# Seven block products, column-major, for the second merge gate's projection

## The reference

```
h = rms_norm(x, norm_g)
... , g_a, g_b = split(h @ w_in)          # g_a and g_b: 1024 columns each
y_a = gelu(u) * mixed(layer_norm(gelu(v))) * silu(z_a)
y_b = sparse_attention(q, k, v, qi, ki, wi) * silu(z_b)   # top 128 keys per query
o_a = y_a @ w_oa ;  o_b = y_b @ w_ob
merged = sigmoid(g_a + b_a) * o_a + sigmoid(g_b + b_b) * o_b
x = x + merged @ w_out
```

## Time and profile before

| | us |
|---|---|
| median of 3 runs | 794.5 (794.45 to 795.74) |
| the profiled execution, its own time | 794.48 |
| its span | 792.7 |
| PE busy | 783.3 (99%) |
| DVE busy | 587.6 (74%) |
| ACT busy | 353.7 (45%) |

### The profile page before, as it was taken

One profiled execution on the slowest core, in us unless ns is written; L12 is line 12 of the kernel. 1 busy time (PEld: TensorE's weight loads), 2 busy tenths in 40 slices (PEclk: granted clock), 3 DMA queues, 4 the chain that ended last, 5 costly groups with the idle time before them and its releaser, 6 DMA issues.

```text
span 792.7 us, 10745 instructions
## 1 busy us (share of the span) xinstructions
PE 783.3 (99%) x3836; PEld 659.2 (83%) x3836; DVE 587.6 (74%) x1026; ACT 353.7 (45%) x658; POOL 110.9 (14%) x101
## 2 busy tenths in 40 slices
PE   7999999999999999999999999999999999999998
PEld 6988888888888888888899888888888888888886
DVE  5779999978766763359986799999786658423895
ACT  6566644341444324434664765433324342335242
POOL 1257510000000000012211674000000000000130
PEclk9999999999999999999999999999999999999999
DMA  9634233223233122275873532323323222224574
GB/s 329 221 114 126 80 107 92 79 70 105 81 106 103 36 81 100 71 226 117 190 236 107 162 86 73 106 81 107 96 67 105 80 80 80 73 88 163 129 144 122
DMA packets 41572, 91.53 MB, mean 115 GB/s; under 512 B 2864, under 2 KB 3056, under 8 KB 41520
## 3 DMA queue, kind: packets, MB, share of 16 engines
q1 hardware_dynamic: 33408, 69.21, 27.8%
q0 software_dynamic: 7824, 21.06, 11.3%
q10 hardware_dynamic: 288, 0.59, 0.2%
HBM read 84.56 MB, written 6.29 MB: 115 GB/s over the span
## 4 chain that ended last, share of the span: by engine, by line
PE 91%; DVE 5%; DMA 2%; ACT 1%; issue 1%; ACTq 0%; DVEq 0%; SPq 0%
PE bank L700 22%; PE bank L702 22%; PE bank L701 22%; PE bank L784 4%; PE bank L736 3%; PE bank L735 3%; PE bank L734 3%; PE bank L674 2%; PE bank L692 2%; PE bank L630 1%; PE bank L683 1%; DMA x_sb<-in_x 1%; PE bank L645 1%; PE bank L644 1%; DVE w_lo L1149 1%; DMA norm_bc<-in_norm_g 1%
## 5 line engine op out<-in xcount | busy, mean ns | idle before, releaser
L1149 DVE TENSOR_TENSOR w_lo<-w_raw,w_hi 128x1024 fp32r<-128x1024 f32 x132 | 172.2, 1319 | 11.7 <-ACT w_hi L867 8.4
L700 PE MATMUL bank<-h_lo,w_hi 128*128 128x512 f32 x448 | 180.6, 403 | 0.0
L702 PE MATMUL bank<-h_hi,w_hi 128*128 128x512 f32 x448 | 174.7, 390 | 0.0
L701 PE MATMUL bank<-h_hi,w_lo 128*128 128x512 f32 x448 | 174.4, 389 | 0.0
L867 ACT ACTIVATE w_hi<-w_raw 128x1024 fp32r<-128x1024 f32 x132 | 135.6, 1056 | 22.3 <-DMA w_raw<-in_w_out 14.0
L700 PE MATMUL bank<-w_lo,h_hi 128*128 128x512 f32 x256 | 100.5, 393 | 0.0
L702 PE MATMUL bank<-w_hi,h_hi 128*128 128x512 f32 x256 | 99.9, 390 | 0.0
L701 PE MATMUL bank<-w_hi,h_lo 128*128 128x512 f32 x256 | 99.8, 390 | 0.0
L701 PEld LDWEIGHTS bank<-h_hi,w_lo 128*128 128x128 f32 x448 | 84.2, 188 | 18.5 <-issue 1.4
L700 PEld LDWEIGHTS bank<-h_lo,w_hi 128*128 128x128 f32 x448 | 84.2, 188 | 18.3 <-issue 1.4
L702 PEld LDWEIGHTS bank<-h_hi,w_hi 128*128 128x128 f32 x448 | 84.1, 188 | 18.1
(11 more groups left out here) (174 smaller groups left out, 1362.6 us busy)
## 6 DMA issues: line engine op xcount, KB each, us to landing
w_raw<-in_w_in SPq DMA_DIRECT2D x96, 512.0 KB, 3.7
w_raw<-in_w_out POOLq DMA_DIRECT2D x16, 512.0 KB, 6.1
w_raw<-in_w_out SPq DMA_DIRECT2D x12, 512.0 KB, 3.4
out<-x_sb POOLq DMA_DIRECT2D x4, 1024.0 KB, 6.4
w_raw<-in_w_oa SPq DMA_DIRECT2D x8, 512.0 KB, 3.4
w_raw<-in_w_ob SPq DMA_DIRECT2D x8, 512.0 KB, 3.3
x_sb<-out POOLq DMA_DIRECT2D x2, 2048.0 KB, 9.3
x_sb<-in_x SPq DMA_DIRECT2D x4, 512.0 KB, 9.1
```

The costliest lines, as they stand in the source:

```text
L700: nc.tensor.matmul(dst, s_h, m_l, start=(n == 0), stop=False)
L701: nc.tensor.matmul(dst, s_l, m_h, start=False, stop=False)
L702: last = nc.tensor.matmul(dst, s_h, m_h, start=False, stop=(n == len(pairs) - 1))
L1149: nc.vector.tensor_tensor(lo, w_raw[:, raw_slot(layer, u)], hi.bitcast(F32), ALU.subtract) \
```

## The change

The `gb` stage has 14 jobs instead of 8 (n = 48 to 61): seven products of blocks, each in two jobs p = 0, 1. h and the gate's weight are cut into 2x2 blocks (256 tokens or 512 channels a side). A job takes four blocks of 128 channels, two tiles of 128 gate columns and three passes: 24 matmuls with 256 moving columns, and fills one bank with two tiles of 256 tokens. The products are a11, a12, s5, s3, s6, s4, a22 in this order. The bank of a11 goes on to take s3, s4 and a22, the bank of a12 (its own after s5 opens it anew) takes s5 and s6. Between products ACT copies a bank to `g_b` (after a11, s5, s3), DVE adds a bank to `g_b` (after a12, s6, s4), and ACT makes the tanh in halves.

Four sums of blocks of h are made by DVE in ten steps (`h_sum_step`), one at the end of each `ga` job and of `oa` jobs 0 and 1. ACT rounds them in `oa` jobs 1, 3, 5, 7 and DVE makes their remainders in `oa` jobs 2, 4, 6 and `gb` job 0.

The stage takes 14 weight units instead of 8; eight of them are accumulated onto a slot by POOL. The roundings and remainders of the units, and those of the `ob` weights, stand in the jobs that `LATE_GATE_UNITS` and `OB_UNITS` list. Attention steps follow `gb` jobs 0, 2, 4, 6; y_b is split in `gb` jobs 8 to 10. Banks of `ob` and `out` are renumbered. The SBUF that software DMA uses for descriptors is cut to 4096 bytes a partition.

```diff
-    ("gb", "w_in", COL["gb"], 4), ("gb", "w_in", COL["gb"] + W512, 4),
+    ("gb", "w_in", COL["gb"], 14),
...
+SEVEN = 14
+UNIT_FIRST = np.cumsum([0] + [SEVEN if g[3] == SEVEN else NQ for g in GROUPS]).tolist()
+UNITS = UNIT_FIRST[-1]
...
+GATE_PRODUCTS = ["a11", "a12", "s5", "s3", "s6", "s4", "a22"]
+H_SUMS = ["s4", "s5", "s3", "s6"]
+H_ROUNDED = ["s5", "s4", "s3", "s6"]
+REGION = [0, 1, 0, 1, 0, 1, 0, 1, 0, 1, 0, 1, 1, 0]
+LATE_GATE_UNITS = dict(scalar=[0, 0, 1, 1, 4, 5, 6, 7, 8, 9], vector=[0, 1, 2, 2, 4, 5, 6, 7, 9, 9])
+OB_UNITS = dict(scalar=[10, 10, 11, 12], vector=[10, 11, 12, 13])
...
+GATE_BANKS = ((0, 2), (1, 6))
+OB_BANKS = [2, 0, 1, 2, 0, 1, 2, 0]
...
-SPLIT_YB = {JOB_GB[4]: [0, 1], JOB_GB[5]: [2], JOB_GB[6]: [3]}
+SPLIT_YB = {JOB_GB[8]: [0, 1], JOB_GB[9]: [2], JOB_GB[10]: [3]}
...
+                return [w[:, 2 * i:2 * i + 2] for w in weights(g)], slot_free(layer, g)
+            name, part = PRODUCTS[i // 2], i % 2
+            pair, k = block_home(g, name)
+            that = job_of if g == OUT_G else gate_job
+            used = dict(a11=FIRST_JOB[g - 1], a12=FIRST_JOB[g - 1], s5=FIRST_JOB[g], s6=FIRST_JOB[g],
+                        s3=that("a11", 1) + 1, s4=that("s5", 1) + 1, a22=that("s6", 1) + 1)[name]
             return [w[:, k.start + 2 * part:k.start + 2 * part + 2] for w in pair], s_job.at(layer, used)
...
+            if g == GB_G:
+                return [GB_U + 4 + i for i, job in enumerate(LATE_GATE_UNITS[engine]) if job == j - JOB_GB[0]] + \
+                    [UNIT_FIRST[g + 1] + i for i, job in enumerate(OB_UNITS[engine]) if job == j - JOB_GB[0]]
...
+                def add_weights(u):
+                    slot = raw_slot(layer, u)
+                    pool.wait_ge(s_wlo.sem, s_wlo.at(layer, u - RAW + 1))
+                    pool.dma_start(w_raw[:, slot], block_weights(layer, u), accum_op=ALU.add) \
+                        .then_inc(s_wadd[slot], 16)
+                for u in range(GB_U, GB_U + SEVEN):
+                    if unit_adds(u):
+                        add_weights(u)
...
+            def gate_b_job(layer, n):
+                name, p = gate_of_job(n)
+                b = bank_of(n)
+                if takes_bank(n):
+                    pe.wait_ge(s_free[b].sem, s_free[b].at(layer, BANK_USE[n]))
+                elif name == "s3":
+                    pe.wait_ge(s_gsnap.sem, s_gsnap.at(layer, p + 1))
+                elif name == "s6":
+                    pe.wait_ge(s_gsnap.sem, s_gsnap.at(layer, 2 + p + 1))
+                elif name == "s4":
+                    pe.wait_ge(s_gsnap.sem, s_gsnap.at(layer, 4 + p + 1))
+                else:
+                    pe.wait_ge(s_gadd.sem, s_gadd.at(layer, 4 + p + 1))
+                if p == 0 and name in H_ROUNDED:
+                    pe.wait_ge(s_hslo.sem, s_hslo.at(layer, H_ROUNDED.index(name) + 1))
+                (w_hi, w_lo), w_k = block_home(GB_G, name)
+                a_hi, a_lo = gate_operand(name)
+                for k in range(HALF_K):
+                    if p == 0 and k % 2 == 0:
+                        pe.wait_ge(s_wlo.sem, s_wlo.at(layer, GB_U + 2 * PRODUCTS.index(name) + k // 2 + 1))
+                    wk, first = w_k.start + k, k == 0 and name in OPENS
+                    for i in range(2):
+                        dst, col = bank[b][:, i * 2 * P:(i + 1) * 2 * P], slice((2 * p + i) * P, (2 * p + i + 1) * P)
+                        nc.tensor.matmul(dst, w_lo[:, wk, col], a_hi[:, k], start=first and i == 0, stop=False, skip_group_check=True)
+                        nc.tensor.matmul(dst, w_hi[:, wk, col], a_lo[:, k], start=False, stop=False, skip_group_check=True)
+                        last = nc.tensor.matmul(dst, w_hi[:, wk, col], a_hi[:, k], start=False, stop=(k == HALF_K - 1),
+                                                skip_group_check=True)
+                last.then_inc(s_job.sem, 1)
...
+            def gate_b_tanh(layer, name, p):
+                half, tokens = dict(a12=(0, top), s6=(1, top), s4=(1, bottom), a22=(0, bottom))[name]
+                n = gate_job(name, p)
+                if name == "a22":
+                    act.wait_ge(s_job.sem, s_job.at(layer, n + 1))
+                else:
+                    act.wait_ge(s_gadd.sem, s_gadd.at(layer, dict(a12=0, s6=2, s4=4)[name] + p + 1))
+                for i in range(2):
+                    d = HALF_K * half + 2 * p + i
+                    dst = tokens(g_b, d)
+                    src = bank[bank_of(n)][:, i * 2 * P:(i + 1) * 2 * P] if name == "a22" else dst
+                    act_.mark(nc.scalar.activation(dst, src, ACT.Tanh, scale=-0.5 if half else 0.5,
+                                                   bias=gate_half[:, KD + d:KD + d + 1]))
+                act_.join(act)
+                act.sem_inc(s_gb.sem, 2)
+                if name == "a22":
+                    act.sem_inc(s_free[bank_of(n)].sem, 1)
...
+            def gate_b_out(layer, n):
+                name, p = gate_of_job(n)
+                if name in ("a11", "s5", "s3"):
+                    gate_b_copied(layer, n)
+                if (name, p) == ("a12", 1):
+                    gate_b_tanh(layer, "a12", 0)
+                if (name, p) == ("s5", 0):
+                    gate_b_tanh(layer, "a12", 1)
+                if (name, p) == ("s6", 1):
+                    gate_b_tanh(layer, "s6", 0)
+                if (name, p) == ("s4", 0):
+                    gate_b_tanh(layer, "s6", 1)
+                if (name, p) == ("s4", 1):
+                    gate_b_tanh(layer, "s4", 0)
+                if (name, p) == ("a22", 0):
+                    gate_b_tanh(layer, "s4", 1)
+                if name == "a22":
+                    gate_b_tanh(layer, "a22", p)
...
+            def h_sum_rounded(layer, name):
+                act.wait_ge(s_hsum.sem, s_hsum.at(layer, H_SUMS.index(name) + 1))
+                if name == "s5":
+                    act.wait_ge(s_job.sem, s_job.at(layer, JOB_GA[-1] + 1))
+                if name == "s6":
+                    act.wait_ge(s_hslo.sem, s_hslo.at(layer, H_ROUNDED.index("s5") + 1))
+                nc.scalar.activation(gate_operand(name)[0], h_sum_raw(name), ACT.Copy,
+                                     scale=-1.0 if name == "s3" else 1.0).then_inc(s_hshi.sem, 1)
...
+                    h_sum_rounded(layer, H_ROUNDED[(n - JOB_OA[1]) // 2])
                 if n in JOB_OB:
...
+            def h_sum_step(layer, step):
+                upper = slice(HALF_K, KD)
+                f = lambda block: block.bitcast(F32)
+                s4, s5, s3, s6 = (h_sum_raw(name) for name in H_SUMS)
+                steps = [
+                    (s4, f(top(h_hi)), f(bottom(h_hi)), ALU.subtract), (s4, s4, f(top(h_lo)), ALU.add),
+                    (s4, s4, f(bottom(h_lo)), ALU.subtract),
+                    (s5, f(bottom(h_hi, upper)), f(bottom(h_hi)), ALU.subtract), (s5, s5, f(bottom(h_lo, upper)), ALU.add),
+                    (s5, s5, f(bottom(h_lo)), ALU.subtract),
+                    (s3, s5, f(top(h_hi)), ALU.add), (s3, s3, f(top(h_lo)), ALU.add),
+                    (s6, s3, f(top(h_hi, upper)), ALU.subtract), (s6, s6, f(top(h_lo, upper)), ALU.subtract)]
+                dst, a, b, op = steps[step]
+                vec.link(dve, nc.vector.tensor_tensor(dst, a, b, op))
+                if step in (2, 5, 7, 9):
+                    dve.sem_inc(s_hsum.sem, 1)
+            def h_sum_remainder(layer, name):
+                hi, lo = gate_operand(name)
+                dve.wait_ge(s_hshi.sem, s_hshi.at(layer, H_ROUNDED.index(name) + 1))
+                nc.vector.scalar_tensor_tensor(lo, h_sum_raw(name), -1.0 if name == "s3" else 1.0, hi.bitcast(F32),
+                                               ALU.mult, ALU.subtract).then_inc(s_hslo.sem, 1)
+            def gate_b_added(layer, n):
+                name, p = gate_of_job(n)
+                if name not in ("a12", "s6", "s4"):
+                    return
+                b = bank_of(n)
+                part = dict(a12=top(g_b, gate_tiles(0, p)), s6=top(g_b, gate_tiles(1, p)),
+                            s4=bottom(g_b, gate_tiles(1, p)))[name]
+                dve.wait_ge(s_job.sem, s_job.at(layer, n + 1))
+                dve.wait_ge(s_gsnap.sem, s_gsnap.at(layer, dict(a12=0, s6=4, s4=2)[name] + p + 1))
+                vec.link(dve, nc.vector.tensor_tensor(part, part, bank[b][:].rearrange("p (i q) -> p i q", i=2), ALU.add))
+                dve.sem_inc(s_gadd.sem, 1)
+                if name != "s4":
+                    dve.sem_inc(s_free[b].sem, 1)
...
                     if n >= min(AFTER_ATT):
                         topk(n)
+                    if n in JOB_GA + JOB_OA[:2]:
+                        h_sum_step(layer, n - JOB_GA[0])
+                    if n in JOB_OA[2::2]:
+                        h_sum_remainder(layer, H_ROUNDED[(n - JOB_OA[2]) // 2])
+                    if n == JOB_GB[0]:
+                        h_sum_remainder(layer, "s6")
...
```

(50 more changed lines are left out.)

111 lines of the change are left out of this document (72 added, 39 removed).

## The result

The changed kernel takes 807.86 us, median of 4 runs (807.0 to 808.3), beside 794.48 for the kernel before: 1.0162 times as long, 95% interval 1.0147 to 1.0177. The direction and both forecast waits were right. The size was not: I said +6.4 us, it is +13.4, outside the range. Rival 4, PE's clock falling behind the new waits, had 5%; it happened, and it makes up the largest part of what is missing.

What follows compares the result with a forecast made beforehand. PE's stream was taken to bound the kernel. Per layer, -4.3 (matmuls) + 4.3 (`oa`) + 3.2 (a22) = +3.2 us, so +6.4 over two layers: 794.5 to 800.9 us, said as 801, range 793.5 to 806.

Steps and rivals of the forecast that it cites:

- both forecast waits: New PE waits per layer: 4.3 us in `oa` for DVE's results, 3.2 us before the first a22 job in `gb`.
- Rival 4: PE's clock falls in the new waits, each of four costing 1.5 to 2 us more: 807 us; chance 0.05.
- Forecast, both waits there and the clock full, 0.62: Main case: both new waits occur and PE keeps full clock, own range 797.5 to 804 us; chance 0.62.
- The matmuls: In `gb`, 336 matmuls of 117 ns replace 192 of 227 ns: gain 4.3 us a layer, bounds 3.6 and 6.3.
- Rival 3: Matmuls in `gb` reach the 111 ns floor, a gain of 6.3 us a layer: 797 us; chance 0.07.
- The `oa` wait: In `oa`, 4.8 us of added DVE work exceeds a 0.94 us margin, so `gb` starts 4.3 us late each layer.
- The a22 wait: Late in `gb`, DVE's queue delays the add to `g_b`; PE stands 3.2 us a layer before the first a22 job.
- ACT idle for 5 us: Sign expected in the changed profile: ACT idle 5 us before the rounding in `gb` job n = 56.
- Nothing lost elsewhere: Copies to `g_b`, other adds and tanh halves in `gb` cost nothing; at most 0.5 to 0.8 us each if uncovered.
- Rivals 1 and 2: First: one wait is absent, 792.3 or 794.5 us, chance 0.14. Second: both are absent, 785.9 us, chance 0.08.
- rival 2: Neither the `oa` nor the a22 wait is there: -4.3 us a layer, 785.9 us, faster; chance 0.08.

Runs made afterwards that it cites:

- x4: Changed kernel with 24 filler matmuls of 256 columns on PE right ahead of its wait for the first a22 add: 804.8 us.
- x7: Kernel before, with only DVE's part of the change added as 14 operations of no use to the result: 805.7 us.
- x5: Kernel before, with only POOL's descriptor space cut to the changed kernel's size: 794.7 us.
- x9: Kernel before, with each 512-column `gb` matmul done as two halves of 256 columns: 799.0 us.
- x6: Changed kernel with all sums of h in `ga`, a22's rounding behind the second s6 job, and POOL's reload of x later: 786.6 us.
- x3: Changed kernel with all sums of h done in `ga` and a22's rounding put behind the second s6 job: 790.8 us.
- x8: Changed kernel with `ob`'s first weight remainder one job later in DVE's order, behind the add for the first a22 job: 808.1 us.
- x2: Changed kernel with the rounding of a22's units put behind the second s6 job: 803.5 us.

## Why the prediction was wrong

**The step that failed** is "Forecast, both waits there and the clock full, 0.62", with the 0.05 for rival 4. I priced a wait at its own length. Behind three of the four waits the clock fell, and PE paid for that after the wait had ended: 1.49 us in `gb` (51.72 against x4's 50.23), 1.0 to 1.2 in `oa` (34.72 against 33.68 in x7, 34.94 against 33.73 in the changed kernel). That is 1.49 + 1.49 + 1.2 = 4.2 of the 6.4 us of span that I missed. My price in rival 4, 1.5 to 2 us a wait, was somewhat high for the 1.0 to 1.5 measured; the chance was far too low. That its 807 lies so near the measured 807.9 is luck: three falls and not four, each cheaper, and the gap filled by the terms below. The evidence on which I gave it 0.05 was that the earlier trace rows show full clock with waits of up to 2.2 us. It held no wait of 3 us at all, so it could not speak against the fall, and it was one execution: of the 17 executions of the kernel before that were timed beside x5, ten had a mean clock of 1.000 and seven a lower one, and the two lowest (0.996 and 0.995) were the two longest, 796.9 and 797.6 us for a median of 794.5.

**The matmuls** were mis-sized. By x9 one costs (53.04 - 50.68 + 192 x 0.227) / 384 = 119.6 ns. That is the line through the earlier trace rows, my 119; I had let two steps of an index stage pull it down to 117. The gain is 3.6 us a layer by x6, not 4.3: 1.4 us in both layers. It is the lower of my own bounds. Rival 3 (111 ns) is out. The Trainium skill's gap (TensorE: Matmul & The Clock Gate, section Back-to-back issue gap) would have given 109 ns at full clock, which the trace does not bear out; its N/1.2 at the lower clock gives 213, and there the trace agrees.

**The `oa` wait**: right in place, cause and nearly in size. x7 makes it without the products, x3 is free of it. With the clock full it costs 4.8 us a layer and not 4.3. The rows show 0.73 + 2.85 + 0.25 = 3.83 us, and each wait costs some 0.26 us more than it shows (x4), which makes 4.6 of the 4.8. The forecast of its parts (0.7 at `oa` job 5, 3.9 in all at the transposes, 0.4 at the next) was 0.73, 3.6 and 0.25. The two layers' 0.5 make 1.0 of the 6.4.

**The a22 wait**: right. 3.2 us forecast, 2.90 shown, 3.16 paid at full clock. DVE's queue came in the written order, and x8 shortened the wait by the 1.15 us of one remainder. I named "ACT idle for 5 us": 5.11.

**Nothing lost elsewhere** held with one exception, a wait of 0.21 us for z_b in the first layer (0.5 paid with the restart). 4.2 + 1.4 + 1.0 + 0.5 - 0.64 (the sooner start of this execution) = 6.5, for the 6.4 missed.

**Rivals 1 and 2** are out as descriptions of this kernel; but x6 is what rival 2 would have been, at 786.6 where I said 785.9. With 3.6 us a layer rival 2 would be 787.3; the 0.7 us that x6 has besides brings the two numbers closer than the sum deserves.

## What to carry to other kernels

A wait put before a TensorE that is always busy costs more than its row: the restart (0.26 us here) and, where the clock falls, the matmuls behind it at half speed for a while (1.0 to 1.5 us for waits of 2.8 to 3 us; nothing where another wait follows at once, as in x8). When a forecast puts new waits there, the clock's fall belongs in the sum, with its chance. A row in which such a wait passed at full clock does not take it out: the first `oa` wait of the changed kernel passed so in one profile and not in the other.

A change that saves matmuls by giving DVE more must first find slots in which DVE had been waiting (here `ga`, one stage earlier). Price a matmul by long streams of like shape, or by a kernel that changes only its shape.

## What the runs showed of the hardware

- The clock's fall is not settled by the wait's length. In the eight long `oa` and `gb` waits of two profiles of one program it fell behind seven, in the first `oa` once and once not. Behind waits of 2.8 to 3.0 us it fell in 13 of 16 cases (both profiles of the changed kernel, x2, x4, x7, x8), behind x8's 1.76 us in one layer of two, behind `ob` waits of 1.4 to 2.5 us (x2, x3) in none of four, and in the first stage behind 1.08 us in the changed kernel's first profile and in x6. What decides stays open.
- Behind a 2 MB transfer issued 1 us ahead on POOL's queue a 512 KB weight transfer on SP's took 6.7 and 7.8 us (x3, the two layers); with the 2 MB held back it took at most 3.9 (x6).
- Matmuls with a new stationary tile, start to start at full clock: 227 ns with 512 moving columns, 119.6 ns with 256 (x9). At the lower clock 213 ns with 256 (changed kernel, 340.26 to 343.25).
